# Expert-choice routing by slot numbers, with each expert's gather between the halves of the down product

## The reference

```python
hn = rms_norm(h, w_norm_ffn)
cap = CAPACITY_FACTOR * T // N_EXPERTS                       # 34
aff = softmax(einsum('btd,de->bte', hn, w_router))           # 16 experts
top_aff, top_idx = top_k(swapaxes(aff, 1, 2), cap)           # each expert picks its 34 tokens
xg = hn[bi, top_idx]
hg = einsum('becd,edf->becf', xg, w_gate)                    # 1024 -> 2048
hu = einsum('becd,edf->becf', xg, w_up)
y = einsum('becf,efd->becd', silu(hg) * hu, w_down)          # 2048 -> 1024
y = y * top_aff[..., None]
h = h + zeros_like(hn).at[bi, top_idx].add(y)
```

## Time and profile before

| | |
|---|---|
| runs | 2507.17, 2507.76, 2512.72 us; median 2507.76 |
| profiled execution, span from first to last instruction | 2505.9 us |
| what lies around the span, taken as median less span | 1.9 us |
| PE, DVE, ACT, POOL busy | 94%, 48%, 29%, 1% of the span |
| mean granted TensorE clock | 0.960 |
| HBM read | 657.40 MB |
| routing (first token block to first product of expert 0) | 521.95 to 550.97 us |
| experts | 550.97 to 1483.74 us |

### The profile page before, as it was taken

How to read it: one execution, slowest core, us unless ns; L and a number is a source line. 1 busy time by engine, 2 the same in 40 slices (tenths; PEclk the granted TensorE clock), 3 DMA queues, 4 the chain that set the end, 5 groups by cost and what they waited for, 6 DMA issues and landing times. The chain is left out here.

```text
span 2505.9 us, 35019 instructions
## 1 busy us (share of the span) xinstructions
PE 2356.9 (94%) x14241; PEld 1581.3 (63%) x14241; DVE 1202.2 (48%) x2445; ACT 722.3 (29%) x1268; POOL 22.5 (1%) x38
## 2 busy tenths in 40 slices
PE   8999999989998988989898979999999999999998
PEld 6786778963222222222222237889999999888887
DVE  5677876631111111111111125248887776788887
ACT  2145556420000000000000012324454444455554
POOL 1000000000000000000000000000000000000000
PEclk9999999989999999999999989899999999999999
DMA  5375555738999999999999982314775555877775
GB/s 169 112 220 185 175 170 171 254 158 362 428 428 427 428 428 428 428 427 428 428 428 428 428 326 69 123 62 152 225 227 180 173 176 180 252 241 242 241 241 163
DMA packets 205424, 677.08 MB, mean 270 GB/s; under 512 B 15072, under 2 KB 137200, under 8 KB 180336
## 3 DMA queue, kind: packets, MB, share of 16 engines
q1 hardware_dynamic: 205296, 675.30, 72.9%
HBM read 657.40 MB, written 17.83 MB: 269 GB/s over the span
## 5 line engine op out<-in xcount | busy, mean ns | idle before, releaser
L1091 PE MATMUL ps<-ring,tokens 128*34 128x512 f32 x1248 | 273.6, 593 | 16.4 <-DMA ring<-in_w_up 16.4
L1269 DVE TENSOR_TENSOR first_room<-first_room,ps 98x512 f32<-98x512 f32 x32 | 21.8, 682 | 503.6 <-PE ps L1091 503.6
L2126 PE MATMUL ps<-m_hi,row_hi 128*128 128x256 f32 x1024 | 256.5, 288 | 0.8 <-ACT peer_s L2192 0.8
L2126 PE MATMUL ps<-m_lo,row_hi 128*128 128x256 f32 x1024 | 250.7, 283 | 0.0
L605 PE MATMUL ps<-u,ring 128*128 128x272 f32 x1024 | 244.7, 395 | 3.0 <-DVE ring L423 2.9
L605 PEld LDWEIGHTS ps<-u,ring 128*128 128x128 f32 x1024 | 191.5, 190 | 46.1 <-issue 7.2
L1091 PE MATMUL ps<-extra_early,tokens 128*34 128x512 f32 x752 | 198.6, 680 | 11.6 <-DMA extra_early<-in_w_gate 9.8
L1091 PEld LDWEIGHTS ps<-ring,tokens 128*34 128x34 f32 x1248 | 72.2, 112 | 215.0 <-issue 186.4
L1108 PE MATMUL ps<-ring,first_room 128*34 128x512 f32 x768 | 181.1, 619 | 25.2 <-DVE first_room L1273 22.9
L2126 PEld LDWEIGHTS ps<-m_hi,row_hi 128*128 128x128 f32 x1024 | 195.7, 191 | 1.6 <-issue 1.0
L2126 PEld LDWEIGHTS ps<-m_lo,row_hi 128*128 128x128 f32 x1024 | 196.1, 191 | 0.0
(11 more groups left out here) (425 smaller groups left out, 3232.0 us busy)
## 6 DMA issues: line engine op xcount, KB each, us to landing
ring<-in_w_down SPq DMA_DIRECT2D x48, 2048.0 KB, 21.6
ring<-in_w_up SPq DMA_DIRECT2D x47, 2048.0 KB, 24.5
extra_early<-in_w_gate SPq DMA_DIRECT2D x31, 2048.0 KB, 18.2
ring<-in_w_gate SPq DMA_DIRECT2D x31, 2048.0 KB, 24.5
ring<-in_w_in SPq DMA_DIRECT2D x36, 1024.0 KB, 5.5
extra_early<-in_w_up SPq DMA_DIRECT2D x16, 2048.0 KB, 25.7
extra_early<-in_w_down SPq DMA_DIRECT2D x16, 2048.0 KB, 25.2
rows<-in_peer_u SPq DMA_DIRECT2D x64, 512.0 KB, 3.8
```

What stands on the lines that cost most here:

```text
L1091: last = pe.matmul(s.ps[HALF * j:HALF * j + CAP, 2 * c + u % 2, :], s.tokens[:, 2 * (u // 2) + k, :], rows[k][:, 1024 * c + 512 * j:1024 * ...
L1269: dve.tensor_tensor(s.hidden[:, c, :], s.silu[:, c, :], s.ps[0:PAIR, 2 * c + 1, :], ALU.mult)\
L2126: pe.matmul(out, hi[:, P * k:P * k + P], m[:, k, :], start=k == 0 and m is s.m2_hi, stop=False)
```

## The change

- Instead of lists of indices, each expert has a row over the 272 tokens: 0 where the token is not picked, else its slot number 1 to 34 (`place_at`: a mask of picked tokens, its running count, their product). The slots are numbered in token order; the affinities are kept as a row as well (`aff_t`).
- The token rows are kept in float32 as one tensor `tok`, no longer as two rounded parts.
- A gather is made for one expert at a time: `hot` holds its 34 columns of zeros and ones (POOL copies them from `onehot`, one expert ahead), PE multiplies (24 matmuls of 34 columns), ACT stores to `tokens` in two halves. `gather(0)` stands ahead of expert 0, and `gather(e + 1)` in expert e behind the first half of the down product.
- Behind that gather two matmuls bring the expert's rows of `place_at` and `aff_t` to 98 partitions (L1140 of the new kernel), and DVE makes `spread` from them in two steps, between the two copies of the transposed `hidden`.
- DVE multiplies both halves of `hidden` first and copies the transposes later.
- Expert 0's units 0 to 5 lie in the ring now, its units 6 to 8 in the three rooms; SP loads them in another order, the same bytes.
- In the mixer each norm sum moves one product ahead, the last but one into the last product, and the router's part comes before the squares. The affinities are turned after three of the six token blocks.

The core of the diff:

```diff
 def expert_place(e, u):
-    q = (u + EXPERT_RING - AHEAD) % EXPERT_RING
-    return q, UNITS // EXPERT_RING * e + (u - AHEAD) // EXPERT_RING + 1
+    i = UNITS * e + u - (AHEAD if UNITS * e + u >= FIRST_ROOM + AHEAD else 0)
+    return i % EXPERT_RING, i // EXPERT_RING + 1
...
         def _(pool):
-            def pick(half, e):
-                pool.wait_ge(products, 8 * e + 8 * EXPERTS // 2 * half + FIRST)
-                pool.tensor_copy(s.tokens[:, :, :], s.picked[half][:, :, bass.ds(e * CAP, CAP)]).then_inc(picked, 1)
+            def mark_row(e):
+                pool.wait_ge(rows_out, e)
+                pool.tensor_copy(s.pick_row[:, :], s.ident[0:EXPERTS, bass.ds(e, 1)].to_broadcast([EXPERTS, PAIR]))\
+                    .then_inc(pick_row, 1)
+
+            def mark_tokens(e):
+                pool.wait_ge(gathered, 2 * e)
+                pool.tensor_copy(s.hot[:, :, :], s.onehot[:, :, bass.ds(e * CAP, CAP)]).then_inc(hot, 1)
...
         def _(pe):
-            def gather(half):
-                for m in range(KT):
-                    i = KT * half + m
-                    if i >= 2:
-                        pe.wait_ge(gathered_out, i - 1)
-                    for j in range(3):
-                        for part in (s.tok_hi, s.tok_lo):
-                            last = pe.matmul(ps[:, 6 + i % 2, 0:HALF_SLOTS], part[:, j, P * m:P * m + P],
-                                             s.onehot[:, j, HALF_SLOTS * half:HALF_SLOTS * (half + 1)],
-                                             start=j == 0 and part is s.tok_hi, stop=j == 2 and part is s.tok_lo)
+            def gather(e):
+                pe.wait_ge(hot, e + 1)
+                for half in range(2):
+                    for m in range(4):
+                        for j in range(3):
+                            last = pe.matmul(gathered_at(half)[:, CAP * m:CAP * m + CAP],
+                                             s.tok[:, j, P * (4 * half + m):P * (4 * half + m) + P], s.hot[:, j, :],
+                                             start=j == 0, stop=j == 2)
                     last.then_inc(gathered, 1)
...
                         last.then_inc(down, 1)
+                    if c == 0:
+                        pe.wait_ge(added, KT * e + FIRST)
+                        if gather_next:
+                            gather(e + 1)
+                        pe.wait_ge(pick_row, e + 1)
+                        pe.wait_ge(tokens_in, 2 * e + (4 if gather_next else 2))
+                        for bank, values in ((6, s.place_at), (7, s.aff_t)):
+                            last = pe.matmul(s.ps[0:PAIR, bank, 0:T], s.pick_row[:, :], values[:, :], start=True, stop=True)
+                        last.then_inc(rows_out, 1)
                 pe.wait_ge(y_out, e + 1)
-                pe.wait_ge(onehot, e + 1)
+                pe.wait_ge(spread, e + 1)
...
         def _(act):
+            def store_tokens(e):
+                for half in range(2):
+                    act.wait_ge(gathered, 2 * e + half + 1)
+                    act.activation(s.tokens[:, 4 * half:4 * half + 4, :], gathered_at(half).rearrange("p (m c) -> p m c", m=4),
+                                   ACT.Copy).then_inc(tokens_in, 1)
...
         def _(dve):
+                for c in range(2):
+                    dve.wait_ge(turned, 2 * e + c + 1 + FIRST)
+                    dve.wait_ge(down, 4 * e + FIRST)
+                    dve.tensor_copy(s.hidden_t[:, c, :, :], s.ps[:, 4, 0:4 * PAIR].rearrange("p (q t) -> p q t", q=4))\
+                       .then_inc(turned_out, 1)
+                    if c == 0:
+                        dve.wait_ge(rows_out, e + 1)
+                        dve.wait_ge(scattered, KT * e + FIRST)
+                        dve.tensor_scalar(s.spread[:, :], s.ps[0:PAIR, 6, 0:T], s.slot_at[0:PAIR, 0:1], None, ALU.is_equal).then_inc(matched, 1)
+                        dve.wait_ge(matched, e + 1)
+                        dve.tensor_tensor(s.spread[:, :], s.spread[:, :], s.ps[0:PAIR, 7, 0:T], ALU.mult).then_inc(spread, 1)
...
             for r in range(ROUNDS):
                 at = slice(8 * r, 8 * r + 8)
-                link(dve.max(s.top[:, at], s.work[:, :]))
-                link(dve.max_index(s.top_at[:, at], s.top[:, at], s.work[:, :]))
-                if r + 1 < ROUNDS:
-                    link(dve.match_replace(s.work[:, :], s.top[:, at], s.work[:, :], -1.0))
+                link(dve.max(s.top[:, at], values))
+                if r == ROUNDS - 1:
+                    link(dve.memset(s.top[:, CAP:8 * ROUNDS], -1.0))
+                link(dve.match_replace(s.work[:, :], s.top[:, at], values, -1.0))
+                values = s.work[:, :]
+            link(dve.tensor_scalar(s.picked[:, :], s.work[:, :], -1.0, None, ALU.is_equal))
+            link(dve.tensor_tensor_scan(s.rank[:, :], s.picked[:, :], s.picked[:, :], 0.0, ALU.add, ALU.max))
+            dve.tensor_tensor(s.place_at[:, :], s.rank[:, :], s.picked[:, :], ALU.mult).then_inc(placed, 1)
```

More of the change, by code:

```diff
@@ L585, in _, with proj @@
         def _(pe):
-            def proj(t):
+            def proj(t, before_lower=None):
                 kind, m, unit, c = tiles[t]
@@ L1016, in experts @@
-    (picked, products, silu, hidden, turned, turned_out, down, y_out, onehot, scattered, added) = (
-        s.sem(f"expert_{k}") for k in names)
+    names = ("rstd3", "std3", "shifted", "exp", "aff", "turned", "aff_t", "placed", "place_t", "marked", "tok", "tok_zero",
+             "tok_out", "slot_at")
+    (rstd3, std3, shifted, exped, aff_ready, turned_aff, aff_t_out, placed, place_t, marked, tok, tok_zero,
+     tok_out, slot_at) = (s.sem(f"route_{k}") for k in names)
+    names = ("hot", "gathered", "tokens", "pick_row", "rows", "products", "silu", "hidden", "turned", "turned_out", "down", "y",
+             "matched", "spread", "scattered", "added", "cleared")
@@ L1018, in experts, with gathered_at @@
+    (hot, gathered, tokens_in, pick_row, rows_out, products, silu, hidden, turned, turned_out, down, y_out,
+     matched, spread, scattered, added, cleared) = (s.sem(f"expert_{k}") for k in names)
     w, load, ps, aff, exp = s.w, s.load_expert_unit, s.ps, s.aff, s.aff_exp
-    HALF_SLOTS = SLOTS // 2
+    place_cols = ps[:, 7, 0:3 * EXPERTS].rearrange("p (j e) -> p j e", j=3)
     def by_block(bank, r):
         return bank.rearrange("t (b k s p) -> t b k s p", b=2, k=2, s=2)[:, r // 2, :, r % 2, :]
-    def tok_part(part, j, q):
-        return part[0:TT[j][1], j, 512 * q:512 * q + 512]
+    def gathered_at(half):
+        return s.ps[:, 6 + half, T:T + 4 * CAP]
@@ L1047, in _ @@
         def _(sp):
-            for i in range(AHEAD, UNITS * EXPERTS - EXPERT_RING):
-                freed(sp, i // UNITS, i % UNITS)
-                load(sp, (i + EXPERT_RING) // UNITS, (i + EXPERT_RING) % UNITS)
+            ringed = [(e, u) for e in range(EXPERTS) for u in range(UNITS) if not in_room(e, u)]
+            for i in range(len(ringed) - EXPERT_RING):
+                freed(sp, *ringed[i])
+                load(sp, *ringed[i + EXPERT_RING])
             for i in range(4):
@@ L1134, in _ @@
             last.then_inc(turned_aff, 1)
-            pe.wait_ge(lists, 1)
-            pe.wait_ge(tok_out, 2)
-            pe.wait_ge(tok_rest, 2)
-            for half in range(2):
-                pe.matmul(ps[:, half, 0:HALF_SLOTS], s.ones[0:EXPERTS, :], s.apart[:, HALF_SLOTS * half:HALF_SLOTS * (half + 1)],
-                          start=True, stop=True).then_inc(index_rows, 1)
-            pe.wait_ge(lists, 2)
-            pe.wait_ge(tok_out, 3)
-            pe.wait_ge(tok_rest, 3)
-            for q, rows in enumerate((s.index2, s.aff2)):
-                last = pe.matmul(ps[0:PAIR, 2, EXPERTS * q:EXPERTS * q + EXPERTS], rows[:, :],
-                                 s.ident[0:EXPERTS, 0:EXPERTS], is_transpose=True, start=True, stop=True)
@@ L1148, in _ @@
-            last.then_inc(lists_t, 1)
-            pe.wait_ge(tok_zero, 2)
-            pe.wait_ge(tok_rest, 6)
-            pe.wait_ge(onehot_ready, 1)
+            for i in range(3, 6):
+                turn_tokens(i)
+            pe.wait_ge(placed, 1)
+            for j, (t0, n) in enumerate(TT):
+                last = pe.matmul(place_cols[0:n, j, :], s.place_at[:, t0:t0 + n], s.ident[0:EXPERTS, 0:EXPERTS],
+                                 is_transpose=True, start=True, stop=True)
+            last.then_inc(place_t, 1)
@@ L1152, in _ @@
+            pe.wait_ge(tok_zero, 1)
+            pe.wait_ge(tok_out, 6)
             gather(0)
             pe.wait_ge(cleared, 1)
+            pe.wait_ge(marked, 2)
+            pe.wait_ge(aff_t_out, 1)
             expert(0)
-            pe.wait_ge(added, KT + FIRST)
-            pe.wait_ge(onehot_ready, 2)
-            gather(1)
-            pe.wait_ge(gathered_out, 2 * KT)
-            with pe.Fori(1, EXPERTS) as e:
+            with pe.Fori(1, EXPERTS - 1) as e:
                 expert(e)
+            expert(EXPERTS - 1, gather_next=False)
```

(10 more changed lines are left out.)

238 lines of the change are left out of this document (104 added, 134 removed).

## The result

| | before | after |
|---|---|---|
| runs, median | 2508.7 us (4 runs, 2507.2 to 2512.7, in the comparison) | 2651.1 us (4 runs, 2648.0 to 2654.1) |
| profiled execution, span | 2505.9 us | 2646.0 us |
| mean granted clock | 0.960 | 0.917 |
| expert 0's first product | 550.97 us | 546.74 us |
| last scatter ends | 1483.74 us | 1621.62 us |

What follows compares the result with a forecast made beforehand. The weight stream was taken as the bound, 58.8 us an expert against PE's 54.5. Added terms made 66.35 us an expert, PE-bound; the stage's end moved +113.9 us, giving 2621.7, said as 2620, range 2550 to 2660.

Steps and rivals of the forecast that it cites:

- forecast A: Expert stage turns from stream-bound to PE-bound, the clock falling during the gather: 66.35 us an expert, 2620 us; chance 0.66.
- B: The gather between the down halves keeps full clock: 62.55 us an expert, about 2564 us; chance 0.17.
- C: Work added between the down halves fits PE's slack, the weight stream stays the bound: 2489 us; chance 0.07.
- signs named for A: Expert stage: experts 64 to 68 us apart, gather 6 to 9 us at both clocks, about 380 GB/s.
- first unit behind the scatter: Start of a later expert: this unit takes 5.73 us at lower clock instead of 3.63, +2.1 us.
- gather, store, read-outs, DVE between the halves: Between the down halves: 48 records 7.3 us, waiting for ACT's store 0.9, two read-out matmuls 1.3, DVE's steps +0.7.
- first unit of the second down half: Right behind the gather and read-outs: starts at half clock, +1.7 us, or 0 if the clock holds.
- The routing: Ahead of the experts: expert 0 starts near 545.9 instead of 550.97 us; outside 543 to 549 would be wrong.
- the top-k: Ahead of the experts: DVE starts it at 527.7 instead of 529.80 us, affinities being turned after three token blocks.
- the mixer's last sums: Mixer's tail: moving a sum forward saves nothing, and the last sum loses cover for DVE's add and ACT's square: +0.7 us.
- Worth 13 us to a stage that waits for the stream: Expert 0's loads: first slot free after one unit, not four; 13 us if stream-bound, nothing otherwise.
- the price of a record: In the gather: weight loads set the pace, 0.115 us a record at full clock, 0.218 at half.

## Why the prediction was right, and where its terms were off

The mechanism was right: the stream bounded the stage with 4.2 us to spare for PE, the change put more than that on PE and made it the bound (the two runs with half the bytes), and forecast A held against B and C. The sum came out 29 us too low, and two of the signs named for A missed narrowly: experts 68.3 us apart, not 64 to 68, and the gather in 5.91 us nearly all at full clock, not 6 to 9 at both. Expert by expert, by first and last records of expert 8 against the second expert of before (52.35 us):

| step | predicted | measured |
|---|---|---|
| first unit behind the scatter | 2.1 | 2.6 |
| first down unit at half clock | 0 | 1.7 |
| gather, store, read-outs, DVE between the halves | 7.3 + 0.9 + 1.3 + 0.7 = 10.2 | 8.65 |
| first unit of the second down half | 1.7 | 2.6 |
| scatter at half clock | 0 | 0.8 |
| wait for `y` | 0 | -0.4 |
| sum over 52.35 | 14.0 | 16.0 |

- The gather was put at 7.3 us, with the clock falling on its way. It took 5.91 (0.123 a record, against the bound of 0.115) and the fall came at its end. The price was paid by what stands behind it. Only in experts 11 and 14 did the fall come in the gather, which took 7.53 and 7.52 us there; in return their first down unit stayed at full clock, and they took 68.2 us like the others.
- The step that failed is the price of the clock: 2.1 us beyond 52.35 and 1.7 behind the gather, with nothing for the first down unit and the scatter. The first unit behind the scatter cost 2.6, the first one behind the gather 2.6, the first down unit 1.7 and the scatter 0.8, 7.7 us instead of 3.8. Before, half clock in the first down unit came in some experts and hid under the stream; after, it came in each from expert 2 on but for 11 and 14. The scatter takes 6.70 us in expert 8 instead of 5.93, where half clock took only its last part. I had not counted that the clock falls three times an expert, ahead of the first down unit too.
- Part of the nearness is luck. What stands between the down halves came out 1.55 us cheaper than said. With that term right and the others as they were, the sum would have been 23 us lower, near 2598, and 53 us off instead of 29.
- Over the stage: the 15 periods sum to 65.14 + 65.02 + 13 x 68.3 = 1018.1 us instead of 995.3, +22.8; the last expert +0.4; expert 0 starts 0.8 later than said; the second block's way up to the last record is 2.2 longer (stage end +137.9, span +140.1), in small steps whose cause no run shows; and the median lies 5.1 us above the span instead of 1.9, since the profiled execution is the shortest of its four (it alone lies 2.0 above its span). 2621.7 + 22.8 + 0.4 + 0.8 + 2.2 + 3.2 = 2651.1.
- The routing was right: expert 0 at 546.74 for 545.9, the top-k at 528.85 for 527.7, the gather 10.43 us for 10.5, and the mixer's last sums 0.9 later (521.18 for 520.29) for 0.7.
- "Worth 13 us to a stage that waits for the stream" was wrong, and with it rival C's 2489: the loads alone brought nothing (ratio 0.9998). It was of no consequence for the forecast. A time near C's was in reach all the same, 2499 without the gathers, where expert 1 starts at 603.3 instead of 612.4.
- On the price of a record the rows decided as said: 0.123 us behind a fresh load of 128 columns at full clock, and 0.217 at half. The first is near what the Trainium skill's page "TensorE: Matmul & The Clock Gate" has in its section "LDWEIGHTS (loading the stationary operand)", a load's columns / 1.2 ns, 107 ns for 128; the second is twice that. It is far from the floor in that page's section "Back-to-back issue gap", some 25 ns for up to 64 columns, a gap that the section itself calls that of a matmul alone, without its load.

## What to carry to other kernels

Before work is moved onto an engine that is "only" second in line, take its time alone (here 54.6 of 58.8 us, shown by loading half the bytes), add the new work at both clocks, and add what the clock takes from the neighbours too. A product with few columns behind each weight load costs the load: batch several users of the same stationary rows (in these runs 136 columns cost no more than 34), and put the batch where PE is slow anyway. A prefetch that starts earlier is worth nothing if the slots are all full before the next consumer frees one; look for the last time that the stream stands still.

## What the hardware showed that I had not expected

- A gather of 48 records of 34 columns ran at or near 1.00, and 48 more behind it at 0.50, though the weight load was busy throughout (5.9 and 10.3 us); with 102 columns it ran as fast (5.60 us), and the clock behind it stayed up in 7 of 15 experts.
- Ahead of expert 0, coming from half clock, 34 columns a record left the clock at 0.50 for all of 10.4 us, while with 136 columns it rose within the 8.6 us of the gather, and with 102 the gather took 8.5 us too.
